# A hybrid decoder layer on one core: the second norm's vectors loaded to 32 partitions and spread by GpSimd, and tile 0 normalised by ScalarE and scaled by GpSimd

## The reference

```python
def _layer_norm(x, g, b):
    xf = x.astype(jnp.float32)
    mu = jnp.mean(xf, axis=-1, keepdims=True)
    var = jnp.mean(jnp.square(xf - mu), axis=-1, keepdims=True)
    y = (xf - mu) * lax.rsqrt(var + LN_EPS) * g.astype(jnp.float32) + b.astype(jnp.float32)
    return y.astype(x.dtype)
...
    ff = _moe(x, router_w, router_b, exp_w_gate, exp_b_gate, exp_w_up, exp_b_up, exp_w_down, exp_b_down)
    x = _layer_norm(DEEPNORM_ALPHA * x + ff, ln2_g, ln2_b)
```

## Time and profile before

| what | us |
|---|---|
| median of 3 runs | 1068.6 (1068.29 to 1069.74) |
| span of the profiled execution | 1066.1 |
| median less span | 2.5 |
| PE busy | 1040.6 (98% of the span) |
| POOL busy | 709.7 (67%) |
| DVE busy | 350.6 (33%) |
| ACT busy | 228.1 (21%) |
| transfers | 424.52 MB, mean 398 GB/s |

### The profile page before, as it was taken

One profiled execution on the slowest core, in us unless ns is written; L12 is line 12 of the kernel. 1 busy time (PEld: TensorE's weight loads), 2 busy tenths in 40 slices (PEclk: granted clock), 3 DMA queues, 4 the chain that ended last, 5 costly groups with the idle time before them and its releaser, 6 DMA issues.

```text
span 1066.1 us, 15284 instructions
## 1 busy us (share of the span) xinstructions
PE 1040.6 (98%) x5384; PEld 421.5 (40%) x5385; DVE 350.6 (33%) x682; ACT 228.1 (21%) x366; POOL 709.7 (67%) x742
## 2 busy tenths in 40 slices
PE   9999999999999999999999999999999999999994
PEld 7776443333333333333333333333333333333331
DVE  2728394333322223232322333322222322222214
ACT  2252054111111111111111111111111111111112
POOL 2001036888888888888887688887888888888201
PEclk9999999999999999999999999999999999999998
DMA  9943949999999999999999999999999999999995
GB/s 310 364 175 130 418 166 389 424 432 430 432 432 432 430 431 431 430 432 433 432 430 430 430 432 433 432 432 429 432 430 432 433 432 431 430 432 430 432 426 188
DMA packets 39720, 424.52 MB, mean 398 GB/s; under 512 B 6175, under 2 KB 6175, under 8 KB 14998
## 3 DMA queue, kind: packets, MB, share of 16 engines
q1 hardware_dynamic: 39584, 424.16, 94.9%
q10 hardware_dynamic: 118, 0.13, 0.0%
HBM read 422.86 MB, written 1.42 MB: 398 GB/s over the span
## 4 chain that ended last, share of the span: by engine, by line
DMA 45%; PE 38%; POOL 11%; DVE 4%; issue 1%; POOLq 0%; ACT 0%; SPq 0%; DVEq 0%
PE bank L1503 20%; POOL ring L512 8%; DMA late_pad<-in_exp_w_gate 7%; DMA area<-in_exp_w_up 7%; DMA late_pad<-in_exp_w_down 7%; DMA area<-in_exp_w_down 7%; DMA late_pad<-in_exp_w_up 7%; DMA area<-in_exp_w_gate 7%; PE bank L1290 6%; POOL ring L513 3%; PE bank L1310 3%; PE bank L1538 2%; PE bank L1268 2%; PE bank L1450 2%; PE bank L1458 1%
## 5 line engine op out<-in xcount | busy, mean ns | idle before, releaser
L512 POOL COPY ring<-area 128x1024 f32<-128x1024 f32 x414 | 414.9, 1041 | 128.7 <-DMA area<-in_exp_w_down 28.4
L1503 PE MATMUL bank<-ring,mixT 128*64 128x512 f32 x2112 | 473.2, 595 | 5.6 <-POOL ring L513 5.2
L1503 PEld LDWEIGHTS bank<-ring,mixT 128*64 128x64 f32 x2112 | 147.8, 137 | 292.3 <-issue 273.4
L1503 PE MATMUL bank<-ring,unit_area 128*64 128x512 f32 x1056 | 233.9, 596 | 0.5 <-ACT unit_area L720 0.5
L513 POOL COPY ring<-area 128x1024 f32<-128x1024 f32 x138 | 143.5, 1040 | 0.0
L1503 PEld LDWEIGHTS bank<-ring,unit_area 128*64 128x64 f32 x1056 | 73.0, 137 | 133.7 <-issue 132.1
L512 POOL COPY ring<-late_pad 128x1024 f32<-128x1024 f32 x102 | 102.5, 1043 | 28.0 <-DMA late_pad<-in_exp_w_gate 7.3
L1148 DVE TENSOR_SCALAR bank<-bank 128x512 f32<-128x512 f32 x33 | 23.1, 700 | 214.3 <-PE bank L1503 214.2
L1175 DVE SCALAR_TENSOR_TENSOR bank<-bank,gate_slot,unit_area 128x512 f32<-128x512 f32 x32 | 24.3, 759 | 181.0 <-ACT unit_area L732 181.0
L718 ACT COPY mixT<-bank 128x512 f32<-128x512 f32 x32 | 18.7, 585 | 241.6 <-PE bank L1450 241.6
L1290 PE MATMUL bank<-xT,ring 128*128 128x320 f32 x256 | 70.0, 433 | 0.0
(11 more groups left out here) (296 smaller groups left out, 779.9 us busy)
## 6 DMA issues: line engine op xcount, KB each, us to landing
area<-in_exp_w_up SPq DMA_DIRECT2D x47, 2048.0 KB, 19.9
area<-in_exp_w_down SPq DMA_DIRECT2D x46, 2048.0 KB, 19.8
area<-in_exp_w_gate SPq DMA_DIRECT2D x45, 2048.0 KB, 19.7
late_pad<-in_exp_w_down SPq DMA_DIRECT2D x12, 2048.0 KB, 19.8
late_pad<-in_exp_w_gate SPq DMA_DIRECT2D x11, 2048.0 KB, 19.7
late_pad<-in_exp_w_up SPq DMA_DIRECT2D x11, 2048.0 KB, 19.8
ring<-in_exp_w_gate SPq DMA_DIRECT2D x6, 2048.0 KB, 20.6
ring<-in_exp_w_up SPq DMA_DIRECT2D x5, 2048.0 KB, 21.2
```

The lines of the kernel that those rows point to most:

```text
L512: g.tensor_copy(ring[:, s, c * D:(c + 1) * D], src(s)[:, c * D:(c + 1) * D])
L1503: last = mm(bank[b][side * UT:(side + 1) * UT, :], lhsT, w[:, c, side * HALF:(side + 1) * HALF], start=m == 2 and hf == 0 and c == 0, stop ...
```

## The change

**The loads.** The six loads of lines 391 and 395 go. In their place SP loads each vector to 32 partitions (128 KB each), after slot 5 of expert 30 and ahead of slot 0 of expert 31. POOL spreads them: partitions 0 to 31 to 32 to 63, then 0 to 63 to 64 to 127, then the pair layout in two copies (64 partitions x 1024 each). It counts these in a new semaphore `ln2_wide`.

**Tile 0.** DVE computes the moments and, new, minus the mean into `shift`. ACT multiplies `shift` by the root and computes root * sum + shift from PSUM, half by half. POOL multiplies each half by g and adds b.

**Tile 1.** As before, except that b is added to the second half by DVE, between the two big instructions of the pair; SP waits for that on `ln2_centred`.

**The last combine** waits for one semaphore of its own in place of two.

```diff
             for e, s in itertools.product((NE - 2, NE - 1), range(NSLOT)):
+                if s == 0 and e == NE - 1:
+                    for v, name in ((ln2_g, "ln2_g"), (ln2_b, "ln2_b")):
+                        sp.dma_start(v[0:NE, :], a[name].partition_broadcast(NE).rearrange("p o n -> p (o n)"))\
+                            .then_inc(S["ln2_in"], 16)
                 if s == 0:
                     used = sp.value_load(units_through[0:1, e - 1:e], min_val=1, max_val=MAXU)
                 sp.wait_ge(freed[s], used)
...
-            sp.wait_ge(slot_loaded[4], 16 * (NE - 1 + PRIOR[4]))
-            for v, name in ((ln2_g, "ln2_g"), (ln2_b, "ln2_b")):
-                sp.dma_start(v[:, :], a[name].partition_broadcast(P).rearrange("p o n -> p (o n)"))\
-                    .then_inc(S["ln2_in"], 16)
-            for v, name in ((pair_g, "ln2_g"), (pair_b, "ln2_b")):
-                for h_ in range(2):
-                    sp.dma_start(v[UT * h_:UT * h_ + UT, :], a[name][:, h_ * HALF:(h_ + 1) * HALF]
-                                 .partition_broadcast(UT).rearrange("p o n -> p (o n)")).then_inc(S["ln2_in"], 16)
...
-                    sp.wait_ge(ln2_ok[t], h_ + 1 if t < 2 else 1)
+                    if t == 1 and h_ == 1:
+                        sp.wait_ge(S["ln2_centred"], 3)
+                    else:
+                        sp.wait_ge(ln2_ok[t], h_ + 1 if t == 0 else 1)
...
-            pool.wait_ge(S["ln2_in"], 96)
-            for t in range(2):
-                for h_ in range(2):
-                    cols = slice(h_ * HALF, (h_ + 1) * HALF)
-                    pool.wait_ge(S["ln2_scaled"], 2 * t + h_ + 1)
-                    g.tensor_tensor(result[:, t, cols], result[:, t, cols], ln2_b[:, cols], ALU.add)\
-                        .then_inc(ln2_ok[t], 1)
+            pool.wait_ge(S["ln2_in"], 32)
+            g.tensor_copy(ln2_both[NE:2 * NE, :], ln2_both[0:NE, :]).then_inc(S["ln2_wide"], 1)
+            pool.wait_ge(S["ln2_wide"], 1)
+            g.tensor_copy(ln2_both[UT:P, :], ln2_both[0:UT, :]).then_inc(S["ln2_wide"], 1)
+            pool.wait_ge(S["ln2_wide"], 2)
+            for h_ in range(2):
+                rows = slice(UT * h_, UT * h_ + UT)
+                g.tensor_copy(pair_both[rows, :, :], ln2_both[rows, :].rearrange("p (m n) -> p m n", m=2)
+                              [:, :, h_ * HALF:(h_ + 1) * HALF]).then_inc(S["ln2_wide"], 1)
+            for h_ in range(2):
+                cols = slice(h_ * HALF, (h_ + 1) * HALF)
+                pool.wait_ge(S["ln2_scaled"], h_ + 1)
+                g.tensor_tensor(result[:, 0, cols], result[:, 0, cols], ln2_g[:, cols], ALU.mult)                    .then_inc(S["ln2_wide"], 1)
+                pool.wait_ge(S["ln2_wide"], 5 + h_)
+                g.tensor_tensor(result[:, 0, cols], result[:, 0, cols], ln2_b[:, cols], ALU.add)\
+                    .then_inc(ln2_ok[0], 1)
+            pool.wait_ge(S["ln2_scaled"], 3)
+            g.tensor_tensor(result[:, 1, 0:HALF], result[:, 1, 0:HALF], ln2_b[:, 0:HALF], ALU.add)\
+                .then_inc(ln2_ok[1], 1)
...
+            act.wait_ge(S["ln2_var"], 1)
+            s_.activation(rstd[:, 0:1], rstd[:, 0:1], ACT.Sqrt).then_inc(S["ln2_rstd"], 1)
+            act.wait_ge(S["ln2_rstd"], 1)
+            settle(s_.mul(shift[:, 0:1], shift[:, 0:1], rstd[:, 0:1]))
+            for h_ in range(2):
+                s_.activation(result[:, 0, h_ * HALF:(h_ + 1) * HALF], sum_bank(0, h_), ACT.Identity,
+                              bias=shift[:, 0:1], scale=rstd[:, 0:1]).then_inc(S["ln2_scaled"], 1)
...
-            dve.wait_ge(S["ln2_in"], 96)
...
+            dve.wait_ge(S["ln2_wide"], 4)
+            dve.wait_ge(S["combined"], 1)
...
+            v.tensor_scalar(shift[:, 0:1], mean_var[:, 0, 0:1], -1.0, None, ALU.mult)
+            v.reciprocal(rstd[:, 0:1], rstd[:, 0:1]).then_inc(S["ln2_var"], 1)
...
             settle(v.scalar_tensor_tensor(pair_result, pair[:, :], mean_var[:, 2, 0:1], pair_g,
                                           ALU.subtract, ALU.mult))
+            dve.wait_ge(S["ln2_scaled"], 4)
+            v.tensor_tensor(result[:, 1, HALF:D], result[:, 1, HALF:D], ln2_b[:, HALF:D], ALU.add)                .then_inc(S["ln2_centred"], 1)
             dve.wait_ge(S["ln2_rstd"], 4)
             v.scalar_tensor_tensor(pair_result, pair_result, rstd[:, 2:3], pair_b, ALU.mult, ALU.add)\
                 .then_inc(ln2_ok[2], 1)
...
             def last_combine():
 
-                pe.wait_ge(S["spread_ok"], n_last + 1)
-                pe.wait_ge(S["y_ok"], n_last + 1)
+                pe.wait_ge(S["last_y_ok"], 1)
```

More of the change, by code:

```diff
@@ L149, in hybrid_layer @@
         result = area[:, 0:3 * D].rearrange("p (t n) -> p t n", n=D)
-        ln2_g, ln2_b = (area[:, SLOTW + i * D:SLOTW + (i + 1) * D] for i in range(2))
-        pair_g, pair_b = (area[:, SLOTW + 2 * D + i * HALF:SLOTW + 2 * D + (i + 1) * HALF] for i in range(2))
+        ln2_both = area[:, SLOTW:SLOTW + 2 * D]
+        pair_both = area[:, SLOTW + 2 * D:SLOTW + 3 * D].rearrange("p (m n) -> p m n", m=2)
+        ln2_g, ln2_b = (ln2_both[:, i * D:(i + 1) * D] for i in range(2))
+        pair_g, pair_b = (pair_both[:, i, :] for i in range(2))
         unit_area = sb("unit_area", [P, 4 * HALF])
@@ L729, in unit @@
                 if not more_to_come:
[L730 removed]
+                    s_.mul(y_last, bank[1][:, :], gate_slot[:, 0:1]).then_inc(S["last_y_ok"], 1)
                     return
@@ L1184, in _ @@
             unit(n_last)
-            dve.wait_ge(S["ln2_in"], 96)
-            for t in range(2):
-                halves = [sum_bank(t, h_) for h_ in range(2)]
-                dve.wait_ge(S["combined"], t + 1)
-                moments(halves, t, P, "ln2_var")
-                for h_ in range(2):
-                    cols = slice(h_ * HALF, (h_ + 1) * HALF)
-                    v.scalar_tensor_tensor(result[:, t, cols], halves[h_], mean_var[:, t, 0:1], ln2_g[:, cols],
-                                           ALU.subtract, ALU.mult).then_inc(S["ln2_centred"], 1)
+            dve.wait_ge(S["ln2_wide"], 4)
+            dve.wait_ge(S["combined"], 1)
+            v.bn_stats(stats[:, 0, 0:6], sum_bank(0, 0))
+            settle(v.bn_stats(stats[:, 0, 6:12], sum_bank(0, 1)))
+            settle(v.bn_aggr(mean_var[:, 0, :], stats[:, 0, :].rearrange("p (a b) -> p a b", b=6)))
+            settle(v.tensor_scalar(rstd[:, 0:1], mean_var[:, 0, 1:2], LN_EPS, None, ALU.add))
+            v.tensor_scalar(shift[:, 0:1], mean_var[:, 0, 0:1], -1.0, None, ALU.mult)
+            v.reciprocal(rstd[:, 0:1], rstd[:, 0:1]).then_inc(S["ln2_var"], 1)
+            dve.wait_ge(S["combined"], 2)
+            halves = [sum_bank(1, h_) for h_ in range(2)]
+            moments(halves, 1, P, "ln2_var")
+            for h_ in range(2):
+                cols = slice(h_ * HALF, (h_ + 1) * HALF)
+                v.scalar_tensor_tensor(result[:, 1, cols], halves[h_], mean_var[:, 1, 0:1], ln2_g[:, cols],
+                                       ALU.subtract, ALU.mult).then_inc(S["ln2_centred"], 1)
             pair = bank[SUM_BANKS[2][0]]
```

18 lines of the change are left out of this document (8 added, 10 removed).

## The result

| | before | changed |
|---|---|---|
| median, same session (15 runs each) | 1068.76 us (1066.66 to 1070.6) | 1071.03 us (1068.67 to 1076.08) |
| ratio, 95% interval | | 1.0025 [1.0016, 1.0034] |
| profiled execution: span | 1066.1 | 1074.3 (its time: 1076.08) |

A forecast was written before the change was run, and what follows sets the result against it. Transfers bound the kernel to 978.35, then PE to the last combine, then the second norm from 1052.48. Terms 0 + 0.4 + 0 + 1.0 + 0 = +1.4 us on 1068.6 gave 1070.0, range 1068.4 to 1071.2.

The forecast's parts named there:

- part 2: Before expert 31: two new loads delay its weights by 1.23 us (or 0.61); PE waits 0.4, bounds 0 and 0.5.
- the smallest slack of 0.8: Expert 31, slot 3's first piece: lands 0.8 to 1.0 us before PE needs it, to be taken off the delay.
- the sign that I had named for being wrong at large: PE stalling by over 1 us, or POOL's copies holding up DVE in the unit before and so the matmuls.
- Part 7: Second norm's end: DVE and POOL instructions on SBUF exclude each other; +1.0 us with POOL's chain, bounds +0.3 and +1.75.
- part 6: Second norm: POOL's chain of multiplications and additions is the new path, ending at 1062.27 without exclusion, before 1061.57.
- The rival in which DVE goes twice: Norm's end: both DVE instructions precede POOL's last addition; +1.75 us, with the stall +2.2, 1070.8; chance 0.18.
- the one without exclusion: Norm's end: DVE and POOL don't hold each other off; +0.3 us, stall 0 to 0.4, about 1069.2; chance 0.22.
- Part 1: Behind all weights: removing the six old loads, 1.5 MB, gives 0, as nothing else waits behind them.
- the cover is thin: Before the second norm: the old loads land at 1051.9, DVE starts at 1052.48, so 0.6 us cover.
- Parts 3, 4, 5 and 8: POOL's copies hidden, 6.2 us; DVE earlier, off the path; ACT's first half ends 1055.7; last combine's single wait saves 0.
- No change that can be measured: Whole kernel: time within 0.2%, 2.1 us, of before; chance 0.80, against slower 0.17 and faster 0.03.

The follow-up runs named there:

- e4: Changed kernel with the second vector loaded to partitions 64 to 95 and six POOL copies in place of four; 1070.47 us, ratio 1.0024 to the kernel before.
- e1: The changed kernel again, without any edit, for a second trace; 1071.83 us, ratio 1.0041 to the kernel before.
- e6: Changed kernel with each vector loaded twice, four loads to 32 partitions ahead of expert 31; 1080.31 us in one run.
- e7: Changed kernel with only the first vector ahead of expert 31, the second behind all weights; 1070.66 us in one run.
- e8: Changed kernel with one operand of each of DVE's last two big instructions in PSUM; 1073.47 us, ratio 1.0040 to the kernel before.
- e3: Kernel before with only the new loads and POOL's four copies, old norm and last combine; 1069.69 us, ratio 1.0022 to the kernel before.
- e5: Changed kernel with both vectors loaded to all 128 partitions, still ahead of expert 31, POOL making only the pair copies; 1070.58 us in one run.
- e9: The kernel before itself, unedited, for a second trace; 1068.09 us in one run.
- e2: Kernel before with only the new norm and the last combine's single wait, six old loads kept; 1069.16 us, ratio 1.0008 to the kernel before.
- e11: Changed kernel with vectors to 128 partitions behind all weights, PSUM operands, stores reordered, one on ACT's queue; 1066.76 us, ratio 0.9995 to the kernel before.

## Why the prediction was wrong, point by point

**The step that failed is part 2, the new loads ahead of expert 31 (+0.4).** The mechanism was right: the loads delay all of expert 31, and PE pays delay less slack. The size of its first term was off. I took 1.23 us for the two loads and had 0.61 as the other bound; they cost 2.7 in the first trace and no less in the others. With the smallest slack of 0.8, 2.7 - 0.8 = 1.9, and the loads-only kernel measured 1.99. The slack itself was well read for slot 3; slot 0, which I didn't look at, has 1.5 (before, it is issued at 1000.61, lands 21.7 later at 1022.3, and is needed at 1023.82), so 2.7 makes a wait of 1.2 there; measured, 1.1. All of PE's waits for weights come to 2.0, so the sign that I had named for being wrong at large, a stall of over 1 us, is there.

What I did wrong was to divide the bytes of the narrow loads by 213 GB/s, the rate of a stretch in which other loads moved too, and to call the result an upper bound. What the loads cost a full queue is the time of their own bytes and of the bytes that it fails to move beside them (0.6 and 2.2 us, above); over 2.7 us the 256 KB come to 97 GB/s. The trace of before could have told me more: three weight loads of 2 MB were issued right behind the six bias loads, from 24.84 on, and the dip is longer than the stretch that I read:

```profile
24.00:32.00 8.00, 8.00 (x31) 5.70 (x30) 5.52 (x11) 2.39 (x9) 1.34 (x5) 1.00 1.13 248
```

Against 433 GB/s these 8 us lack 1.5 MB, or 3.4 us; with 1.8 for the 0.79 MB of the bias loads themselves that makes 5.2 for six, so an estimate of 1.7 for two. Small loads of other shapes are in it too, and it is still too low, but it lies above my upper bound. Then the upper end should have been left wide.

The estimate that I worked out from the Trainium skill (SBUF — State Buffer, Door 1: The DMA port swizzle), 1.2 us, failed with it; the measurement decides. e4 spread the two loads over two groups of partitions, and that gave 0.5 back; since each of them still went to 32 partitions, it says little of the page's figure for one such load.

**What no part held is the clock.** In the changed kernel's two traces the waits for weights are followed by 3.4 us at 1.2 GHz, worth 1.5 to 1.7 us (8.64 and 8.80 for a product of 7.11). Without a filler it was seen in five of the eight traces of kernels with loads ahead (changed, e1, e6, e7, e8), not in e3, e4, e5, nor in the kernels with no loads ahead (before, e9, e2, e11). The medians hold it only in part: weights 2.0 and norm 0.9, less the 0.1, make 2.8, the measured change is 2.7 (1.7 to 3.6), and the traces' 4.4 lies above it. Nor is it shown that the waits for weights bring it: e7 had hardly any and fell, e3 and e5 had them and didn't. The mean clock of every timed run is on record and leans the same way (0.9948 over 23 runs of the changed kernel, 0.9954 over 60 of the kernel before; such a stretch would take an estimated 0.0016 off a run), but the 12 runs of e3 have 0.9958, and e9, with a full clock in this place, has 0.994. In what share of the runs the clock falls, and why, stays open.

**Part 7, DVE and POOL in each other's way (with part 6, +1.0): right.** Measured +0.93, by the order forecast: L1233 behind POOL's fourth, POOL's last behind L1233, L1235 behind that. That the number came so close is in part luck. I had 0.3 for POOL's longer chain and 0.7 for the waiting; e8, which has the chain without the waiting, is 0.47 above before, and the waiting made the other 0.46. e8 shows the cause, since the same instructions with one operand in PSUM take 0.69 and 0.74. The rival in which DVE goes twice and the one without exclusion both fall. The Trainium skill (SBUF — State Buffer, Who interferes with whom) names two SBUF inputs of the DVE instruction as the condition, beside a GpSimd instruction that reads SBUF; e8 agrees, with 0.69 against 1.48.

**Part 1, the old loads go (nothing).** Right for the trace of before. That the cover is thin was right too: in e2 it failed, for 0.5 us. So the change takes away a cost that the old loads can have, seen in one trace (with the new norm); how many runs of the kernel before pay it isn't known.

**Parts 3, 4, 5 and 8.** POOL's copies are hidden: e3 has them all, and the tail of before. The 1.04 us that I took for one stands in this row of the page, not in the earlier trace rows; in the changed trace the four take 6.0 us, from 1024.34 on.

```profile
L513 POOL COPY ring<-area 128x1024 f32<-128x1024 f32 x138 | 143.5, 1040 | 0.0
```

Line 1225 took 0.32 in place of 0.89. ACT's two halves came some 0.7 apart and POOL's five instructions started 1.22 to 1.34 apart (forecast 1.22 to 1.35); the turns then made the last one 1.71 long. The last combine's single wait, which I had at nothing within 0 to 0.1, gives 0.1: PE's wait in front of it is 0.87 in the three traces with the old wait (before, e3, e9) and 0.78 or 0.79 in the ten with the new one. One reading of the chain was short: between the last landing, 978.35, and PE's lead stand POOL's copies, to 982.73; nothing in the sum hangs on it.

**The chances.** "No change that can be measured" had 0.80, slower 0.17, and slower it is, if barely. The sum with the measured delay is 1.9 + 1.0 = 2.9, 1071.5, beyond my upper end of 1071.2. The median, 1071.03, lies just inside it, which is luck: the four medians of the kernel before on record differ by up to 0.9 us.

## What to carry to other kernels

A small load is not priced by its bytes once it stands in a full queue: measure it there, or put it behind the last load that anything waits for. Where the weights land only 0.8 us before PE needs them, a delay of 2.7 costs the difference; that it costs the clock as well was seen in some traces and isn't shown as its effect. Work that is moved from one of DVE and POOL to the other gains only if their big instructions don't both have all operands in SBUF at the same time; an operand in PSUM took that waiting away here, and with it half of the tail's loss (0.46 of 0.93).

## What the runs showed of the hardware

- A load of 128 KB to 32 partitions costs the full queue of 2 MB loads 1.2 to 1.35 us (slot 3's landing: one 1.2, two 2.7, four 5.2, in one trace each; other traces with two have up to 3.8). Two loads of 512 KB to 128 partitions cost slot 0 2.6 (slot 3 3.7, in one trace), so four times the bytes for about the same. While the narrow loads pass, the DMA share stays at 0.92 to 1.09 and the rate falls to 289 GB/s; beside the wide ones it stays at 428. Whether it is the partitions or the small number of rows that makes it was not separated; two groups of partitions gave back only 0.5.
- Waits of 1.1, 0.2, 1.5 and 0.5 us, with busy stretches in between, were followed by 3.4 us at half the clock. Much the same waits were not followed by it in another trace (e3), and it came with hardly any wait for weights in e7.
- DVE's additions of 512 columns take 1.48 and 1.75 us beside POOL's with all operands in SBUF, POOL's own 1.71; with one operand in PSUM 0.69, 0.74 and 1.26.
- The last stores of e11, which leave close together from two queues, land after 2.7 to 2.9 us in place of 2.0 to 2.4 (one trace).
- The part ahead of the start point ends between 981.7 and 986.7 in different executions of kernels that are nearly the same up to there. Landings in mid-stream scatter by up to 1.5 us (e2, e5, e8). Both stay unexplained, and both are larger than some of the effects looked for.
